# Recurrent squares summed over a sequence's four units on POOL, and over the features once per sequence on TensorE

## The chip, the cores and the metric

The kernel runs on one core of a Trainium2 chip. A core has five engines that the text names: PE (TensorE, matrix products; PEld is its weight load), DVE (VectorE), ACT (ScalarE), POOL (GpSimd) and SP (SyncE, which issues DMAs). They run their own instruction lists in order and meet only at semaphores. The metric is device time in microseconds (us), lower is better. Three runs of the kernel before took 1675.21, 1675.7 and 1678.19 us, median 1675.7. Its profiled execution has a span of 1672.1 us from the first to the last instruction.

## The reference, cut to what matters

Two sequences of 1024 tokens with 1024 features go through one layer: a layer norm, a mixer and a mixture of experts. The mixer runs attention on one half of the features and a gated linear recurrence (RG-LRU) in both directions on the other half, 512 features. The recurrence's output is normed by the root of its mean square over the 512 features, and that mean square is what the change computes in another way:

```python
h_fwd = rg_lru_scan(xc, lru_wa[0], lru_ba[0], lru_wx[0], lru_bx[0], lru_lambda[0], False)
h_bwd = rg_lru_scan(xc, lru_wa[1], lru_ba[1], lru_wx[1], lru_bx[1], lru_lambda[1], True)
lru = (h_fwd + h_bwd) * jax.nn.gelu(y_lru.astype(jnp.float32))
merged = jnp.concatenate([rms_norm(attn, attn_out_g, LN_EPS),
                          rms_norm(lru, lru_out_g, LN_EPS)], axis=-1).astype(h.dtype)
# rms_norm(x, g, eps): xf * rsqrt(mean(square(xf), axis=-1) + eps) * g
return merged @ w_out
```

## The kernel before, in words

The program runs in stages one after another: `project_xy` (input norm, projection of the recurrent half, convolution), `qkv_lru` (projection to queries, keys and values, and the recurrence), `attend`, the routing, the experts, and a last norm. The change is in `qkv_lru` (about 235 to 482 us of the profile) and in the first few instructions that `attend` does on DVE.

`qkv_lru` carries two jobs side by side. The first is the projection of 16 token tiles of 128 tokens. For a tile t, PE does `front(t)` (48 products into `pj`, lines 110 to 112), ACT copies and squares it (lines 875 to 882), DVE norms it and applies the rotary angles (lines 1018 to 1048) with POOL doing the swapped half (`swap`, line 1100), ACT and POOL split it into a high and a low part (`split`, lines 890, 891 and 1108, 1109), and PE transposes it (`back(t)`, line 829). The second job is the recurrence, in eight units: unit n is a sequence (units 0 to 3 the first, 4 to 7 the second) and one block of 128 features. The features lie on the partitions and the 1024 tokens along the free axis. PE computes the gates (line 841), ACT their tanhs and decays (lines 927 to 945), DVE does three wide products (lines 989, 996, 998), two scans (lines 1004, 1005) and the output (lines 1011, 1014), ACT squares the output into `r[n % 2][:, 1]` (`squares_of_output`, line 868), and PE sums those squares over the 128 features: `sums` (line 799) uses a 128-token piece of the squares as weights and a column of ones as the moving operand, so that the sums come out with one token per partition, 8 columns for 8 pieces. ACT copies these columns into `lru_sums` (line 864), and `attend` adds the four units of a sequence on DVE (line 1552) ahead of an inverse square root.

The order of all this is written out by hand. `GROUPS` lists nine groups g = 0 to 8: tile 0, then tiles (1, 2), (3, 4) up to (13, 14), then tile 15. In group g, PE does the fronts of its tiles, and at the end of the last front the `sums` of unit g - 2; then it does the backs of the tiles of group g - 1 and the gates of unit g. DVE in group g does the second rotation of the tiles before, the wide products and scans of unit g - 1, the norms of the group's tiles, the output of unit g - 1, and the first rotation. ACT squares the output of unit g - 1 as the last thing of group g. POOL in group g does `split` for each tile of the group before and then `swap` for each of its own. After the last group DVE scans unit 7, ACT squares its output, PE sums it (`last_sums`) and ACT copies the sums; then the stage ends, and all engines meet before `attend` starts.

Of the kernel before, what the change touches and what calls it, by code (L numbers as in the profile page):

```python
# [30 lines left out]
ALU = mybir.AluOpType  # L31
ACT = mybir.ActivationFunctionType
AX = mybir.AxisListType.X
# [81 lines left out]
def build(nc, x, ln_in_g, ln_in_b, w_in, conv_w, conv_b, lru_wa, lru_ba, lru_wx, lru_bx, lru_lambda,  # L115
# [13 lines left out]
    with ExitStack() as whole:  # L129
# [4 lines left out]
        with ExitStack() as kept:  # L134
# [3 lines left out]
            v_all = sb("v_all", [P, NT, KVW])  # L138
            lru_sums = sb("lru_sums", [P, SEQS * FT, TPS])

# [487 lines left out]
def qkv_lru(nc, raw, w_hi, w_lo, spare, q_g, k_g, rope, identr, ht_hi_dram, ht_lo_dram, k_hi, k_lo, v_all, q_dram,  # L628
# [11 lines left out]
    with ExitStack() as ctx:  # L640
# [5 lines left out]
        NU = len(UNITS)  # L646

        TILES = [NT - 1, NT - 2] + list(range(NT - 2))
        turned_last = lambda t: [v[:, 1, :].rearrange("p (j k n) -> p j k n", j=2, k=KD)[:, t % 2] for v in (k_hi, k_lo)]
# [37 lines left out]
        i = spare[:, 0:2 * SEQ].rearrange("p (d t) -> p d t", d=2)  # L687
        th = sb("lru_th", [P, 2, SEQ])

        pj = [ps(f"pj{u}", [P, 1024]) for u in range(2)]  # L690
# [39 lines left out]
        squared = sem("lru_squared")  # L730
        last_sums = sem("last_sums_done")
        block = ctx.enter_context(nc.Block())
        by_head = lambda v: v.rearrange("p (h d) -> p h d", h=NH)
# [59 lines left out]
        def _(pe):  # L793

            def sums(n, out):
                pe.wait_ge(ones_made, 1)
                pe.wait_ge(squared, n + 1)
                for c in range(TPS):
                    last = pe.matmul(out[:, SUMS + c:SUMS + c + 1], r[n % 2][:, 1, c * P:(c + 1) * P], ones[:, 0:1],
                                     start=True, stop=True)  # L800
                return last

            def front(t, unit=None):
                u = t % 2
                c = (c_hi[u], c_lo[u]) if t >= 2 else turned_last(TILES[t])
                if t >= 2:
                    pe.wait_ge(c_in[u], 32 * (t // 2))
                    pe.wait_ge(v_done, t - 1)
                for a, b in ((0, QW), (QW, QKVW)):
                    for k in range(KD):  # L810
                        last = three_pass(pe, pj[u][:, a:b], (c[0][:, k, :], c[1][:, k, :]),
                                          (w_hi[:, k, a:b], w_lo[:, k, a:b]), k == 0, k == KD - 1)
                if unit is not None:
                    last = sums(unit, pj[u])
                last.then_inc(pj_done, 1)
# [41 lines left out]
            back(NT - 1, (0, 1, 2))  # L857
            sums(NU - 1, pj[0]).then_inc(last_sums, 1)

        @block.scalar  # L860
        def _(act):

            def keep_sums(n, u):
                return act.activation(lru_sums[:, n, :], pj[u][:, SUMS:SUMS + TPS], ACT.Copy)

            def squares_of_output(n):
                act.wait_ge(out_done, n + 1)
                act.activation(r[n % 2][:, 1], ys[:], ACT.Square).then_inc(squared, 1)

            def square(t, unit=None):  # L870
                u = t % 2
                act.wait_ge(pj_done, t + 1)
                if t >= 2:
                    act.wait_ge(ss_done, t - 1)
                act.activation(sq[u], pj[u][:, 0:QKW], ACT.Square).then_inc(sq_done, 1)
                if t >= 2:
                    act.wait_ge(a_done, t - 1)
                    act.wait_ge(b_done, t - 1)
                act.activation(xr[u], pj[u][:, 0:QKW], ACT.Copy).then_inc(copied, 1)
                if unit is not None:  # L880
                    keep_sums(unit, u)
                act.activation(v_all[:, TILES[t], :], pj[u][:, QKW:QKVW], ACT.Copy).then_inc(v_done, 1)

# [33 lines left out]
            def gate_tanhs(n, pair):  # L917
# [5 lines left out]
                if not of_input and n >= 2:  # L923
                    act.wait_ge(out_done, n - 1)
                for b in (2 * pair, 2 * pair + 1):
                    act.wait_ge(gates_done, GH * n + b + 1)
# [52 lines left out]
            act.wait_ge(last_sums, 1)  # L979
            keep_sums(NU - 1, 0)  # L980
            act.wait_ge(q_stored, 16 * NT)
# [90 lines left out]
        def _(pool):  # L1072
# [31 lines left out]
            def split(t):  # L1104
# [5 lines left out]
                                   k_st[u][:, 0].bitcast(F32), ALU.subtract).then_inc(lo_done, 1)  # L1110

            for g, group in enumerate(GROUPS):
                for t in GROUPS[g - 1] if g else []:
                    split(t)
                for t in group:
                    swap(t)
# [9 lines left out]
def attend(nc, w_out, attn_g, lru_g, ln_g, ln_b, router_wg, router_bg, router_we, router_be, ident,  # L1126
# [14 lines left out]
    with ExitStack() as ctx:  # L1141
# [394 lines left out]
        def _(dve):  # L1536
# [3 lines left out]
            dve.wait_ge(ones_made, 3)  # L1540
            LRU_LINKS = 2 + RSQRT_LINKS_WIDE
            EARLY = LRU_LINKS + 1 + RSQRT_LINKS_WIDE
# [7 lines left out]
            def lru_norms():  # L1550
                link = Chain(dve, dve_link)
                link(dve.tensor_reduce(lru_tmp[:].rearrange("p (s c) -> p s c", s=SEQS),
                                       lru_sums[:].rearrange("p (s f) c -> p s c f", s=SEQS), AX, ALU.add))
                link(dve.tensor_scalar(lru_var[:], lru_tmp[:], ALPHA ** 2 / LW, LN_EPS * ALPHA ** 2, ALU.mult, ALU.add))
                rsqrt(dve, link, lru_var[:], rl[:], lru_tmp[:], wide=True)
# [1096 lines left out]
```

## Time and profile before

| what | value |
|---|---|
| median of three runs | 1675.7 us |
| span of the profiled execution | 1672.1 us |
| median less that span | 3.6 us |
| instructions in the profile | 29383 |
| busy over the span | PE 1504.5, PEld 1273.7, DVE 1096.2, ACT 912.6, POOL 491.1 us |
| granted PE clock, mean | 0.949 |

The span runs from the first instruction to the last; the 3.6 us are what the runs' median has beyond it. The busy times are averages over stages with different limits: over the whole span PE is busy for 90% and DVE for 66%, and inside `qkv_lru` the two are near each other. So the shares of the whole say little about one stage, and the rows further down are read by stage.

### The profile page before, as it was taken

Reading aid. Unit: us, or ns where it says so; the run is one execution under the profiler, and the core shown is the slowest. Engines: PE = TensorE matmul, PEld = TensorE weight load, DVE = VectorE, ACT = ScalarE, POOL = GpSimd, SP = SyncE. Lnnn points to the kernel's source line nnn. Section 1 sums busy time; section 2 is a strip of 40 time slices with the busy share of each in tenths; the row PEclk is TensorE's granted clock in tenths of the full one; section 3 lists DMA queues with packets and bytes.
Section 4 is the critical chain, followed back from the end, with each engine's and each line's share of the span. In section 5 each row is a group of like instructions: output and inputs, shape, how many; then the busy total and the mean of one; then the engine's idle time right before and its main releaser. Section 6 shows DMA issues by size and latency. Waiting matters only on the chain. (4 is left out here: it accounts for less than half of the span.)

```text
span 1672.1 us, 29383 instructions
## 1 busy us (share of the span) xinstructions
PE 1504.5 (90%) x8921; PEld 1273.7 (76%) x8923; DVE 1096.2 (66%) x2047; ACT 912.6 (55%) x1524; POOL 491.1 (29%) x343
## 2 busy tenths in 40 slices
PE   5999989999858999999999999996799999999940
PEld 5999967677747888888888888883587788777830
DVE  7787538999978776767767777767454433444237
ACT  3444437878847555555555565543365544555325
POOL 1212125565620111111111111121454353454318
PEclk9999999999959999999999999995799999999975
DMA  8855543444242111111111111116489777786566
GB/s 277 302 210 200 195 145 117 169 160 168 101 159 83 58 57 57 56 56 61 65 69 64 56 56 57 45 39 227 166 250 277 214 205 202 220 255 185 112 197 268
DMA packets 118771, 245.02 MB, mean 147 GB/s; under 512 B 18082, under 2 KB 71330, under 8 KB 118692
## 3 DMA queue, kind: packets, MB, share of 16 engines
q1 hardware_dynamic: 88752, 156.44, 26.6%
q0 software_dynamic: 12528, 45.62, 11.3%
q10 hardware_dynamic: 17412, 41.96, 6.5%
q8 instruction: 44, 0.72, 0.2%
q14 instruction: 35, 0.29, 0.0%
HBM read 149.61 MB, written 94.37 MB: 146 GB/s over the span
## 5 line engine op out<-in xcount | busy, mean ns | idle before, releaser
L1570 DVE TENSOR_TENSOR d_probs_t_lo<-d_pt_ps,d_probs_t_hi 128x512 fp32r<-128x512 f32 x256 | 164.3, 684 | 103.4 <-ACT d_probs_t_hi L1491 102.6
L1491 ACT ACTIVATE d_probs_t_hi<-d_pt_ps 128x512 fp32r<-128x512 f32 x256 | 139.3, 596 | 152.5 <-PE d_pt_ps L1347 146.1
L1713 POOL TENSOR_TENSOR d_h_tile<-d_s_tile,d_ln_g_b 128x512 f32<-128x512 f32 x30 | 38.6, 1285 | 576.7 <-ACT d_s_tile L1509 545.9
L1548 DVE TENSOR_REDUCE d_neg_max<-d_s_ps 128x1 f32<-128x1024 f32 x128 | 155.6, 1216 | 2.6 <-PE d_s_ps L1336 2.6
L110 PE MATMUL acc<-k_hi,wl_hi 128*128 128x256 f32 x512 | 146.4, 286 | 4.4 <-DVE k_lo L526 4.4
L110 PE MATMUL e_a_ps<-up_hi,e_xt_hi 128*128 x336 | 138.1, 411 | 8.3 <-DVE e_xt_lo L2358 4.2
L111 PE MATMUL acc<-k_lo,wl_hi 128*128 128x256 f32 x512 | 145.5, 284 | 0.0
L112 PE MATMUL acc<-k_hi,wl_lo 128*128 128x256 f32 x512 | 145.4, 284 | 0.0
L1474 ACT ACTIVATE d_probs<-d_s_ps,d_neg_max 128x1024 f32<-128x1024 f32 x128 | 143.3, 1119 | 3.5 <-DVE d_neg_max L1548 3.5
L1365 PE MATMUL d_ot_ps<-d_probs_t_hi,d_v_split 128*128 128x256 f32 x512 | 130.1, 292 | 8.0 <-DVE d_probs_t_lo L1570 5.8
L1347 PE MATMUL d_pt_ps<-ident,d_probs 128*128 128x128 f32 x1024 | 134.0, 274 | 3.3 <-ACT d_probs L1474 3.2
L111 PE MATMUL e_a_ps<-up_lo,e_xt_hi 128*128 x336 | 134.2, 399 | 0.0
L112 PE MATMUL e_a_ps<-up_hi,e_xt_lo 128*128 x336 | 134.1, 399 | 0.0
L1347 PEld LDWEIGHTS d_pt_ps<-ident,d_probs 128*128 128x128 f32 x1024 | 117.7, 141 | 13.2 <-ACT d_probs L1474 5.3
L1365 PE MATMUL d_ot_ps<-d_probs_t_lo,d_v_split 128*128 128x256 f32 x512 | 125.1, 282 | 0.0
L1335 PE MATMUL d_s_ps<-k_hi,d_q_tile 128*128 128x512 f32 (+1 forms) x256 | 113.2, 442 | 4.5 <-DMA d_q_tile<-q_dram 4.5
L2185 POOL DMA_INDIRECT e_xg<-h_dram,e_ix x45 | 45.1, 1003 | 225.9 <-ACT e_yt L2312 123.9
L1365 PEld LDWEIGHTS d_ot_ps<-d_probs_t_hi,d_v_split 128*128 128x128 f32 x512 | 97.3, 190 | 16.7 <-issue 16.7
L1336 PE MATMUL d_s_ps<-k_lo,d_q_tile 128*128 128x512 f32 (+1 forms) x256 | 102.4, 400 | 0.0
L110 PEld LDWEIGHTS acc<-k_hi,wl_hi 128*128 128x128 f32 x512 | 98.2, 192 | 5.0 <-DVE k_lo L526 5.0
L110 PE MATMUL d_m_ps<-d_wo_hi,d_m_hi 128*128 128x512 f32 x240 | 99.4, 414 | 0.0
L111 PEld LDWEIGHTS acc<-k_lo,wl_hi 128*128 128x128 f32 x512 | 98.3, 192 | 0.0
(394 smaller groups left out, 4040.0 us busy)
## 6 DMA issues: line engine op xcount, KB each, us to landing
up_raw<-in_exp_w SPq DMA_DIRECT2D x32, 1024.0 KB, 8.6
down_raw<-in_exp_w SPq DMA_DIRECT2D x16, 1024.0 KB, 14.0
h_dram<-v_all ACTq DMA_DIRECT2D x16, 512.0 KB, 3.4
ht_hi_dram<-k_hi ACTq DMA_DIRECT2D x8, 1024.0 KB, 4.3
ht_lo_dram<-k_lo ACTq DMA_DIRECT2D x8, 1024.0 KB, 6.8
q_dram<-wq_raw ACTq DMA_DIRECT2D x16, 512.0 KB, 3.2
d_q_tile<-q_dram SPq DMA_DIRECT2D x16, 512.0 KB, 3.7
d_h_tile<-h_dram SPq DMA_DIRECT2D x16, 512.0 KB, 3.2
```

The lines of the kernel that those rows point to most:

```text
L110: pe.matmul(out, lhs[0], rhs[0], start=first, stop=False)
L111: pe.matmul(out, lhs[0], rhs[1], start=False, stop=False)
L112: return pe.matmul(out, lhs[1], rhs[0], start=False, stop=last)
L1335: pe.matmul(out, q_t[u][:, h, :], k_hi[:, h // GQ, keys], start=True, stop=False)
L1336: last = pe.matmul(out, q_t[u][:, h, :], k_lo[:, h // GQ, keys], start=False, stop=True)
L1347: last = pe.transpose(pt_ps[c][:, j, :], pr[h % 2][:, k * P:(k + 1) * P], ident[:])
L1365: last = pe.matmul(ot_ps[:, 0:2 * P], vs[:, s * TPS + k, h // GQ].rearrange("p c d -> p (c d)"), part[:, k].rearrange("p e t -> p (e t)"), ...
L1474: act.activation(pr[h % 2][:], s_ps[h % 2][:], ACT.Exp, bias=nm[:, u, h:h + 1], accum_out=rsum[:, u, h:h + 1]).then_inc(p_done, 1)
L1491: act.activation(pt_hi[:, c * HALF:(c + 1) * HALF, h % 2], pt_ps[c][:], ACT.Copy).then_inc(pth_done[c], 1)
L1548: dve.tensor_reduce(nm[:, u, h:h + 1], s_ps[h % 2][:], AX, ALU.max, negate=True).then_inc(nm_done, 1)
L1570: dve.tensor_tensor(pt_lo[:, part, h % 2], pt_ps[c][:], pt_hi[:, part, h % 2].bitcast(F32), ALU.subtract)\
L2185: pool.indirect_dma_start(xg[u][:], None, h1_dram, bass.IndirectOffsetOnAxis(ix[u][:, 0:1], 0))\
```

## The change

The squares of a sequence's four units are added up elementwise before PE sums them over the features.

- ACT writes the squares of the first unit of each sequence (units 0 and 4) straight into a new buffer `sq_sum` of 128 x 1024, and those of the others into `r` as before.
- POOL adds the squares of units 1, 2, 3, 5 and 6 into `sq_sum` (`add_squares`), between the two splits of groups 3, 4, 5, 7 and 8.
- PE sums `sq_sum` once for the first sequence, at the end of the last front of group 5. For the second sequence, at the stage's end, each of the 8 columns takes two products, one on `sq_sum` (units 4 to 6) and one on the squares of unit 7, accumulated.
- ACT copies the sums twice in place of eight times; its writes to a buffer that POOL still has to read wait for the add. `attend` no longer adds four units (line 1552), and `lru_sums` is smaller.

```diff
+        TO_ADD = [n for n in range(NU - 1) if n % FT]
+        ADDS = [len([n for n in TO_ADD if n < FT * (seq + 1)]) for seq in range(SEQS)]
+        sq_sum = sb("lru_square_sum", [P, SEQ])
@@ tensor
-            def sums(n, out):
+            def sums(seq, out):
+                own = seq == SEQS - 1
                 pe.wait_ge(ones_made, 1)
-                pe.wait_ge(squared, n + 1)
+                pe.wait_ge(added, ADDS[seq])
                 for c in range(TPS):
-                    last = pe.matmul(out[:, SUMS + c:SUMS + c + 1], r[n % 2][:, 1, c * P:(c + 1) * P], ones[:, 0:1],
-                                     start=True, stop=True)
+                    last = pe.matmul(out[:, SUMS + c:SUMS + c + 1], sq_sum[:, c * P:(c + 1) * P], ones[:, 0:1], start=True, stop=not own)
+                    if own:
+                        if c == 0:
+                            pe.wait_ge(squared, NU)
+                        last = pe.matmul(out[:, SUMS + c:SUMS + c + 1], r[(NU - 1) % 2][:, 1, c * P:(c + 1) * P], ones[:, 0:1],
+                                         start=False, stop=True)
...
-                if unit is not None:
-                    last = sums(unit, pj[u])
+                if unit == FT - 1:
+                    last = sums(0, pj[u])
...
-            sums(NU - 1, pj[0]).then_inc(last_sums, 1)
+            sums(1, pj[0]).then_inc(last_sums, 1)
@@ scalar
             def squares_of_output(n):
                 act.wait_ge(out_done, n + 1)
-                act.activation(r[n % 2][:, 1], ys[:], ACT.Square).then_inc(squared, 1)
+                if n == FT:
+                    act.wait_ge(summed, 1)
+                act.activation(r[n % 2][:, 1] if n % FT else sq_sum[:], ys[:], ACT.Square).then_inc(squared, 1)
...
                 if not of_input and n >= 2:
                     act.wait_ge(out_done, n - 1)
+                    if n - 2 in TO_ADD:
+                        act.wait_ge(added, TO_ADD.index(n - 2) + 1)
@@ gpsimd
+            def add_squares(n):
+                pool.wait_ge(squared, n + 1)
+                if n % FT > 1:
+                    pool.wait_ge(added, TO_ADD.index(n))
+                pool.tensor_tensor(sq_sum[:], sq_sum[:], r[n % 2][:, 1], ALU.add).then_inc(added, 1)
+
             for g, group in enumerate(GROUPS):
                 for t in GROUPS[g - 1] if g else []:
                     split(t)
+                    if g - 2 in TO_ADD and t == GROUPS[g - 1][0]:
+                        add_squares(g - 2)
@@ attend, vector
-                link(dve.tensor_reduce(lru_tmp[:].rearrange("p (s c) -> p s c", s=SEQS),
-                                       lru_sums[:].rearrange("p (s f) c -> p s c f", s=SEQS), AX, ALU.add))
-                link(dve.tensor_scalar(lru_var[:], lru_tmp[:], ALPHA ** 2 / LW, LN_EPS * ALPHA ** 2, ALU.mult, ALU.add))
+                link(dve.tensor_scalar(lru_var[:], lru_sums[:].rearrange("p s c -> p (s c)"), ALPHA ** 2 / LW, LN_EPS * ALPHA ** 2, ALU.mult, ALU.add))
```

On POOL, in group 3, the order before is split of tile 3, split of tile 4 (`q_st` and `k_st` are the low parts of queries and keys), then the swaps:

```order
L1108 TENSOR_TENSOR q_st<-wq_raw,q_st 128x8x64
L1109 TENSOR_TENSOR k_st<-wq_raw,k_st 128x256
L1108 TENSOR_TENSOR q_st<-wq_raw,q_st 128x8x64
L1109 TENSOR_TENSOR k_st<-wq_raw,k_st 128x256
L1100 TENSOR_TENSOR wq_raw<-wq_raw,rope_gain 128x16x16 x2
```

After the change one instruction stands between the two splits:

```order
L1124 TENSOR_TENSOR k_st<-wq_raw,k_st 128x256
L1131 TENSOR_TENSOR lru_square_sum<-lru_square_sum,lru_r 128x1024
L1123 TENSOR_TENSOR q_st<-wq_raw,q_st 128x8x64
L1124 TENSOR_TENSOR k_st<-wq_raw,k_st 128x256
L1115 TENSOR_TENSOR wq_raw<-wq_raw,rope_gain 128x16x16 x2
```

The second split of the group is now queued behind a 128 x 1024 addition.

On PE the end of the stage before is the back of tile 15 (`tr`) and then the eight sums of unit 7, each of which the chip runs as two instructions:

```order
L829 MATMUL tr1<-identr,q_st1 128x128 x4
L829 MATMUL tr0<-identr,q_st1 128x128 x4
L829 MATMUL tr1<-identr,k_st1 128x128 x4
L799 MATMUL pj0<-ones_b,lru_r1 128x1 x8
```

After the change each column takes a pair (the first pairs and the last are shown here by three):

```order
L806 MATMUL pj0<-ones_b,lru_square_sum 128x1
L810 MATMUL pj0<-ones_b,lru_r1 128x1
L806 MATMUL pj0<-ones_b,lru_square_sum 128x1
L810 MATMUL pj0<-ones_b,lru_r1 128x1
L806 MATMUL pj0<-ones_b,lru_square_sum 128x1
L810 MATMUL pj0<-ones_b,lru_r1 128x1
```

Sixteen products stand there where eight stood, and the six other groups of eight that PE had at the ends of fronts (groups 2, 3, 4, 6, 7 and 8) are gone; the one of group 5 stays, on `sq_sum`.

## Rows read from the trace of the kernel before

**Rows 1.** Busy time by window: PE, PEld, DVE, ACT, POOL, clock, DMA share, GB/s.

```profile
300.00:325.00 25.00, 24.52 (x143) 19.99 (x142) 24.47 (x19) 20.11 (x30) 16.18 (x12) 1.00 0.46 170
```

**Rows 2.** DVE's waits from 255 to 477 us: total, times, longest.

```profile
DVE lru_th L996 <- ACT lru_th L945: 8.0, 2, 6.9
DVE wq_raw L1048 <- POOL wq_raw L1100: 3.3, 8, 1.3
```

**Rows 3.** Timeline of DVE: start, duration, line, operation, [idle before <- releaser].

```profile
294.65 1.51 DVE L1018 TENSOR_REDUCE ss<-wq_raw 128x10 f32<-128x640 f32 x2
...
314.81 2.29 DVE L998 TENSOR_TENSOR spare<-spare,lru_th 128x2048 f32<-128x2048 f32 x1
317.14 3.25 DVE L1004 TENSOR_TENSOR_SCAN lru_r<-lru_r,spare 128x1024 f32<-128x1024 f32 x1
320.31 2.74 DVE L1005 TENSOR_TENSOR_SCAN lru_r<-lru_r,spare 128x1024 f32<-128x1024 f32 x1
322.97 1.51 DVE L1018 TENSOR_REDUCE ss<-wq_raw 128x10 f32<-128x640 f32 x2
...
425.76 2.29 DVE L996 SCALAR_TENSOR_TENSOR lru_th<-lru_r,lru_th 128x2048 f32<-128x2048 f32 x1 [1.07 <-ACT lru_th L945]
...
467.90 2.29 DVE L1004 TENSOR_TENSOR_SCAN lru_r<-lru_r,spare 128x1024 f32<-128x1024 f32 x1
```

**Rows 4.** Timeline of PE: the sums, what follows them, and group 3's later parts.

```profile
288.54 1.84 PE L799 MATMUL pj<-ones_b,lru_r 128*128 128x1 f32 x16
290.24 0.85 PE L829 MATMUL tr<-identr,q_st 128*128 128x128 f32 x8
...
317.28 1.84 PE L799 MATMUL pj<-ones_b,lru_r 128*128 128x1 f32 x16
...
323.79 1.20 PE L829 MATMUL tr<-identr,q_st 128*128 128x128 f32 x8
```

**Rows 5.** Timelines of POOL and ACT in the same group.

```profile
315.15 3.09 POOL L1108 TENSOR_TENSOR q_st<-wq_raw,q_st 128x512 fp32r<-128x512 f32 x1 [4.72 <-ACT k_st L891]
318.19 2.71 POOL L1109 TENSOR_TENSOR k_st<-wq_raw,k_st 128x256 fp32r<-128x256 f32 x1
...
310.34 1.04 ACT L868 ACTIVATE lru_r<-lru_y 128x1024 f32<-128x1024 f32 x1
```

**Rows 6.** The stage before: POOL's 128x1024 adds and DVE beside them.

```profile
100.07 5.64 POOL L326 TENSOR_TENSOR v_all<-v_all,ln_in_b_b 128x1024 f32<-128x1024 f32 x2 [17.43 <-DVE v_all L522]
...
101.05 2.36 DVE L553 TENSOR_SCALAR neg_lam<-lam_t 128x8 f32<-128x8 f32 x1
103.44 2.31 DVE L554 TENSOR_TENSOR abs_lam<-lam_t,neg_lam 128x8 f32<-128x8 f32 x1
```

**Rows 7.** Lines by form: a small DVE operation alone, the last stage's POOL adds.

```profile
L94 DVE TENSOR_SCALAR ms<-ms 128x20 f32<-128x20 f32 x6 | 1.1, 176 | 0.2
...
L2610 POOL TENSOR_TENSOR up_raw<-up_raw,c_b_b 128x1024 f32<-128x1024 f32 x7 | 16.3, 2360 | 0.2
```

**Rows 8.** Timeline of the stage's end, all engines.

```profile
475.02 1.23 DVE L1014 TENSOR_TENSOR lru_y<-lru_y,lru_r 128x1024 f32<-128x1024 f32 x1
...
476.85 1.06 ACT L868 ACTIVATE lru_r<-lru_y 128x1024 f32<-128x1024 f32 x1
...
478.05 3.54 PE L799 MATMUL pj<-ones_b,lru_r 128*128 128x1 f32 x16 [1.85 <-ACT lru_r L868]
```

**Rows 9.** Timeline of the first microseconds of `attend`.

```profile
483.09 0.27 DVE L1552 TENSOR_REDUCE d_lru_tmp<-lru_sums 128x16 f32<-128x64 f32 x1
...
488.29 1.23 DVE L1548 TENSOR_REDUCE d_neg_max<-d_s_ps 128x1 f32<-128x1024 f32 x1 [2.22 <-PE d_s_ps L1336]
```

**Rows 10.** Windows around the stage's end (columns as in rows 1).

```profile
456.00:457.00 1.00, 0.19 (x2) 0.11 (x1) 1.00 (x1) 0.77 (x2) 1.00 (x2) 1.00 0.84 283
...
458.00:459.00 1.00, 0.00 (x0) 0.00 (x0) 1.00 (x2) 0.58 (x2) 1.00 (x1) 0.50 0.00 0
...
490.00:495.00 5.00, 4.11 (x14) 3.20 (x15) 5.00 (x5) 3.54 (x7) 0.00 (x0) 0.50 0.87 181
```

More of the change, by code:

```diff
@@ L138, in build @@
             v_all = sb("v_all", [P, NT, KVW])
-            lru_sums = sb("lru_sums", [P, SEQS * FT, TPS])
+            lru_sums = sb("lru_sums", [P, SEQS, TPS])
             with ExitStack() as front:
@@ L731, in qkv_lru @@
         last_sums = sem("last_sums_done")
+        added = sem("lru_squares_added")
+        summed = sem("lru_squares_summed")
         block = ctx.enter_context(nc.Block())
@@ L863, in keep_sums @@
             def keep_sums(n, u):
-                return act.activation(lru_sums[:, n, :], pj[u][:, SUMS:SUMS + TPS], ACT.Copy)
+                return act.activation(lru_sums[:, n, :], pj[u][:, SUMS:SUMS + TPS], ACT.Copy).then_inc(summed, 1)
             def squares_of_output(n):
                 act.wait_ge(out_done, n + 1)
-                act.activation(r[n % 2][:, 1], ys[:], ACT.Square).then_inc(squared, 1)
+                if n == FT:
+                    act.wait_ge(summed, 1)
+                act.activation(r[n % 2][:, 1] if n % FT else sq_sum[:], ys[:], ACT.Square).then_inc(squared, 1)
             def square(t, unit=None):
@@ L879, in square @@
                 act.activation(xr[u], pj[u][:, 0:QKW], ACT.Copy).then_inc(copied, 1)
-                if unit is not None:
-                    keep_sums(unit, u)
+                if unit == FT - 1:
+                    keep_sums(0, u)
                 act.activation(v_all[:, TILES[t], :], pj[u][:, QKW:QKVW], ACT.Copy).then_inc(v_done, 1)
@@ L979, in _ @@
             act.wait_ge(last_sums, 1)
-            keep_sums(NU - 1, 0)
+            keep_sums(1, 0)
             act.wait_ge(q_stored, 16 * NT)
@@ L1540, in _ @@
             dve.wait_ge(ones_made, 3)
-            LRU_LINKS = 2 + RSQRT_LINKS_WIDE
+            LRU_LINKS = 1 + RSQRT_LINKS_WIDE
             EARLY = LRU_LINKS + 1 + RSQRT_LINKS_WIDE
```

## The prediction

> **What bounds the kernel now.** I read busy time by window first, since the page's shares are means over stages. In the middle of the stage that the change edits, PE is busy for 24.52 of 25 us and DVE for 24.47 [rows 1]. Both look full, and PE's clock is at its full level of 2.4 GHz. Only one of them can set the pace, so I read next who waits for whom. From 255 us, where DVE takes up the products of unit 0, to 477 us DVE waits for ACT 8.0 us in two waits, of which 6.9 come at the very start, and for POOL 3.3 us in eight small ones [rows 2]. So behind the start it idles 1.1 us for ACT [rows 3] and 3.3 for POOL in over 200 us, and never for PE. The timelines give the two rates. PE's sums start 28.74 us apart (288.54 and 317.28) [rows 4]; DVE's squares start 28.32 us apart (294.65 and 322.97) [rows 3]. DVE began 6.1 us behind PE and gains a little on it in each group; once, at 425.76, it catches up and waits 1.07 us for the chain that starts at PE. PE's own lead can be read too: PE takes up tile 4's transposes at 323.79 [rows 4], while POOL has delivered them at 318.19 + 2.71 = 320.90 [rows 5], 2.9 us earlier, and POOL's delivery is paced by DVE. So the stage has two clocks that nearly agree. Take 2 to 3 us from PE and it stands at a DVE-paced handover; add to DVE and the stage's end moves by as much. At the end only DVE counts: its last output ends at 476.25, ACT squares, PE sums, ACT copies, and the stage is over [rows 8].
>
> **PE's part inside the groups.** Eight sums are 16 instructions, 1.70 us from the first to the next operation (288.54 to 290.24) [rows 4]. Six of these go, 10.2 us of PE. But PE is not what ends last there. DVE has nothing shorter in its list, and the only idle time of DVE that a faster PE and ACT take away is the 1.07 us of [rows 3]. I take -1.1 us for the removal of 10.2. The rest becomes PE's waiting: for POOL's second split of the group, and for the tanhs that wait for DVE's scans. ACT loses six copies of 8 columns each; DVE waits for ACT only in that same 1.07 us, so they are in it already.
>
> **POOL's part.** Five additions of 128 x 1024 f32. POOL itself has room for them: it stands idle 4.72 us ahead of the second split [rows 5], and an addition takes 2.36 us alone [rows 7]. ACT's squares of unit 1 are ready at 311.38 [rows 5], behind POOL's first split, so the order holds nobody up for long. What costs is DVE. Look at 314.81 to 323.05 [rows 3] beside [rows 5]. POOL's operation on 128 x 512 starts at 315.15, makes no headway until DVE's product ends at 317.10 and takes 3.09 us; the scan behind that product then takes 3.25 us, against 2.29 for a scan that meets nothing (at 467.90) [rows 3], 0.96 more. The next scan takes 2.74, 0.45 more, beside the tail of POOL's 128 x 256 operation. They don't share: one holds and the other stands still. For the size in question the trace has a direct case in the stage before. Beside two POOL adds of 128 x 1024 that take 5.64 us together, two DVE operations on 8 columns take 2.36 and 2.31 us [rows 6]; one on 20 columns alone takes 0.18 [rows 7]. Each add took 2.18 and 2.13 us from DVE. Where the five new adds would start, DVE is in its wide products, each with two operands in SBUF, and has no idle time that could take them. The last add, of unit 6 in group 8, meets DVE's small norm operations, which is the case of [rows 6] itself. I take 2.14 us each, 10.7 in all. From below the price is 0 if none of them meets DVE, and 1.92 each (twice the 0.96 of a half-size operation) by the next nearest row; from above 2.36 each, the whole add, 11.8. A gain is excluded: an add shortens nothing on DVE.
>
> The Trainium skill ("SBUF — State Buffer", section "Who interferes with whom") has a rule that speaks against this change: DVE and GpSimd share one pair of SBUF ports under an exclusive lock, and a DVE instruction with two SBUF inputs blocks, or is blocked by, a GpSimd instruction that reads SBUF, for the whole of it. The trace agrees in kind (the 0.96 us and the 2.13 us above). By the rule taken to the letter each add would cost its whole 2.36 us, 1.1 us more in the sum than by the row.
>
> **New waits.** PE's sums of the first sequence in group 5 wait for the add of unit 3, with the transposes and gates behind them. ACT's first gate tanh of groups 3, 4, 5 and 7 waits for the add; behind it stand ACT's decays, for which DVE waits later. PE's own work is now 28.7 - 1.7 = 27.0 us a group, and DVE's 28.3 + 2.1 = 30.4, so PE has 3.4 us a group to lose, and the add starts as soon as the DVE product then running ends. Both waits fit into that. I take 0. If the cover is gone, they cost what the next case below says.
>
> **The stage's end.** The last sums start when ACT has squared unit 7 [rows 8]. Before, 16 instructions followed, 3.54 us, 0.221 each, at half clock. Now two of 32 may run ahead of the wait, 30 follow: 14 more, 14 x 0.221 = 3.1 us, with nothing beside them. The bound below: the clock comes back inside the sequence, at 1.70 / 16 = 0.106 each that is 1.5 us; and since PE has then worked for longer before `attend`, whose first products still run at half clock at 490 to 495 [rows 10], it may give back 1.5 us there, so 0. I take 3.1, the row of this very place.
>
> **The first instructions of `attend`.** DVE's addition of 0.27 us goes [rows 9], but DVE waits 2.22 us for PE at 488.29, so it is hidden: 0. Were that cover gone, it would gain 0.3.
>
> **The sum.** -1.1 + 10.7 + 3.1 = +12.7 us on the profiled span of 1672.1, so 1684.8; the median lies 3.6 us above that span, and 1675.7 + 12.7 = **1688.4 us**, 0.76% slower. By the bounds: 5 x 1.92 - 1.1 + 0 = +8.5 (1684.2) to 11.8 + 3.1 = +14.9 (1690.6), the latter without the gain of 1.1.
>
> **Rivals.**
> 1. *The adds meet nobody.* They slide into moments in which DVE uses one SBUF operand, as its reductions do (1.51 us for two) [rows 3]. Then -1.1 + 3.1 = +2.0, 1677.7. For it: ACT and POOL have more slack than DVE, so the adds may settle elsewhere. Against: a reduction is shorter than an add, and POOL takes its operand as soon as it can [rows 5].
> 2. *PE is the pace after all, and the result is faster.* PE's period of 28.74 is the longer of the two [rows 3, 4]. If DVE's surplus could be made up inside its group, say because its blocked time today is due to how POOL falls against it, all of 10.2 would come back: -10.2 + 3.1 = -7.1, 1668.6. It decides from the point where an add takes less than 0.4 us from DVE, the difference of the two periods. Against it stands [rows 6].
> 3. *PE's waits lower its clock.* In [rows 10] the clock goes from full to half within 2 us of PE running dry (456 to 459). PE now waits up to 3.4 us in a group. If it runs at half clock for some 10 us of the next fronts, it loses 5, of which 3.4 are slack, so 1.6 us in each of four groups: 6.4 more, 1694.8. For it: the row. Against: the waiting comes in two pieces with transposes between, and DVE needs PE's tiles only some 10 us later. The Trainium skill ("TensorE: Matmul & The Clock Gate", section "Part 1: The HAM clock gate") says that an idle PE is put back to 1.2 GHz; rows 10 agree.
>
> **How the numbers follow.** The forecast gets 0.76, rival 1 gets 0.09, rival 2 gets 0.06, rival 3 gets 0.09. A measurement of this kernel can tell 0.2%, 3.4 us, from no change. The forecast and rival 3 are slower by more than that; rival 1 is within it; rival 2 faster. That gives faster 0.06, same 0.09, slower 0.85. The range for 8 in 10 goes from 1680, where three of the five adds are hidden and the clock comes back in the last sums (-1.1 + 4.3 + 1.5 = +4.7, 1680.4), to 1692, half way to rival 3.
>
> **What the new profile would show.** Right: DVE full from 255 us to its last output, its squares about 30.4 us apart in the four groups with adds and 28.3 in group 6; in each of the five groups one DVE operation, or two, longer by 2.1 us beside POOL's new line; POOL's add between 2.4 and 4.7 us; PE waiting 2 to 4 us a group for POOL or ACT; 32 last sums in about 7 us; the stage's end some 12 to 13 us later, and nothing changed behind it. Wrong: DVE operations of unchanged length beside the adds, squares still 28.3 apart, or DVE waiting for ACT or PE in the middle groups.

## The result and the profile after

The changed kernel takes a median of 1686.99 us (1682.68 to 1688.56, four runs), the kernel before, run beside it, 1676.49 us (1675.21 to 1678.19, four runs). The ratio is 1.0056 with an interval of 1.0039 to 1.0073: slower, by about 10.5 us. The forecast was 1688.4, or 0.76% slower, which is just above the upper end of that interval. The profiled execution has a span of 1684.6 us against the forecast's 1684.8; before it was 1672.1.

The whole time is a sum over many parts, most of which the change does not touch, so I measure the stage by itself: from DVE's first pair of squares (266.31 us before, 266.37 after) to the first ACT operation of `attend` (482.81 and 495.73). Before this is 216.50 us, after 229.36, **12.86 more; the forecast's sum was 12.7**.

DVE's timeline of the changed kernel in group 3, columns as in [rows 3]. The lines are numbered anew: L1011 is the old L996, L1013 the old L998, L1019 and L1020 the two scans, L1033 the squares.

```profile
312.59 4.48 DVE L1011 SCALAR_TENSOR_TENSOR lru_th<-lru_r,lru_th 128x2048 f32<-128x2048 f32 x1
317.11 3.25 DVE L1013 TENSOR_TENSOR spare<-spare,lru_th 128x2048 f32<-128x2048 f32 x1
320.39 2.70 DVE L1019 TENSOR_TENSOR_SCAN lru_r<-lru_r,spare 128x1024 f32<-128x1024 f32 x1
323.02 2.26 DVE L1020 TENSOR_TENSOR_SCAN lru_r<-lru_r,spare 128x1024 f32<-128x1024 f32 x1
325.20 1.51 DVE L1033 TENSOR_REDUCE ss<-wq_raw 128x10 f32<-128x640 f32 x2
```

POOL's timeline beside it: the new addition, then the second split.

```profile
311.54 3.39 POOL L1131 TENSOR_TENSOR lru_square_sum<-lru_square_sum,lru_r 128x1024 f32<-128x1024 f32 x1 [1.02 <-ACT lru_r L881]
315.23 2.98 POOL L1123 TENSOR_TENSOR q_st<-wq_raw,q_st 128x512 fp32r<-128x512 f32 x1 [0.30 <-ACT k_st L904]
318.17 2.77 POOL L1124 TENSOR_TENSOR k_st<-wq_raw,k_st 128x256 fp32r<-128x256 f32 x1
```

Read against [rows 3] and [rows 5]: the addition begins while DVE is in the product ahead, and ends at 314.93. The product behind takes 4.48 us; the operation that meets no one takes 2.29. POOL then starts its second split where it did before (315.23 against 315.15), so the split's two holds fall on the next product and the first scan instead of on the two scans. They cost the same as before: 3.25 and 2.70 where it was 3.25 and 2.74. Only the addition's hold is new. This group's squares start 30.48 us after those of group 2 (294.72), against 28.32 before. From each group to the next it is 30.48, 30.49, 30.45, 28.32 and 30.48 us up to group 7, and the one at the old distance ends in group 6, which has no addition.

In group 8 POOL's addition comes during another product, which has 2.19 us still to go, and holds the next one. First POOL's row, then DVE's:

```profile
462.91 4.39 POOL L1131 TENSOR_TENSOR lru_square_sum<-lru_square_sum,lru_r 128x1024 f32<-128x1024 f32 x1
```

```profile
465.13 4.31 DVE L1013 TENSOR_TENSOR spare<-spare,lru_th 128x2048 f32<-128x2048 f32 x1
```

Less that lead it takes 4.39 - 2.19 = 2.20 us; in group 3 the product ahead had 1.13 us to go, and 3.39 - 1.13 = 2.26. DVE's product is held 2.02 us here and 2.19 there.

DVE's waits from 255 to 490 us, as in [rows 2]. The wait of 1.07 us for ACT is gone, the one at the start and POOL's eight remain:

```profile
DVE lru_th L1011 <- ACT lru_th L960: 6.9, 1, 6.9
DVE wq_raw L1063 <- POOL wq_raw L1115: 3.3, 8, 1.2
```

PE's waits over the same stretch. PE has 10 us less to do and 12.9 us more time, and waits:

```profile
PE tr L840 <- POOL k_st L1124: 23.9, 4, 10.3
PE tr L840 <- ACT wq_raw L913: 5.3, 7, 1.6
PE gp L852 <- ACT spare L942: 4.3, 6, 1.6
...
PE pj L806 <- POOL lru_square_sum L1131: 0.2, 1, 0.2
```

None of these reaches DVE. Of the 23.9 us for POOL's `k_st`, 23.0 fall behind PE's last front, where the kernel before has 11.7; inside the groups it is 0.9 us, once. The last line is the new wait of the first sequence's sum for POOL's third addition: 0.2 us, once, at 376. PE's clock shows two dips, in windows of the length of [rows 1] (columns as there); one is below, the other in 375 to 400 us, also to 0.93:

```profile
325.00:350.00 25.00, 23.46 (x119) 18.30 (x120) 24.13 (x29) 19.98 (x30) 18.28 (x13) 0.93 0.38 139
```

The stage's end answers to [rows 8]. First DVE's last output and ACT's squares, then PE's first pairs, the last one, and ACT's copy with its wait:

```profile
484.96 1.23 DVE L1029 TENSOR_TENSOR lru_y<-lru_y,lru_r 128x1024 f32<-128x1024 f32 x1
...
485.94 0.55 PE L806 MATMUL pj<-ones_b,lru_square_sum 128*128 128x1 f32 x2
...
486.79 1.06 ACT L881 ACTIVATE lru_r<-lru_y 128x1024 f32<-128x1024 f32 x1
...
487.90 0.58 PE L810 MATMUL pj<-ones_b,lru_r 128*128 128x1 f32 x2 [1.41 <-ACT lru_r L881]
...
493.89 0.56 PE L810 MATMUL pj<-ones_b,lru_r 128*128 128x1 f32 x2
494.49 0.18 ACT L875 ACTIVATE lru_sums<-pj 128x8 f32<-128x8 f32 x1 [6.65 <-PE pj L810]
```

Two instructions run ahead, at 485.94, thirty follow from 487.90 to 494.45: 0.218 us each. ACT waited 3.72 us for the sums before and waits 6.65 now, 2.93 more. The clock stays at half over all of it and into `attend` (windows, columns as in [rows 10]):

```profile
490.00:495.00 5.00, 4.46 (x21) 4.37 (x21) 0.00 (x0) 0.18 (x1) 0.00 (x0) 0.50 0.00 0
```

### The profile page after: what moved, and what is told of

It is laid out like the page before. It is cut to its first block and busy times, and to the rows that moved or that the text cites. A ratio compares the mean times of both kernels' runs of the same rounds, so it can differ in the third digit from the quotient of the medians.

```text
span 1684.6 us, 29220 instructions
## 1 busy us (share of the span) xinstructions
PE 1502.6 (89%) x8842; PEld 1268.3 (75%) x8843; DVE 1107.0 (66%) x2046; ACT 913.6 (54%) x1518; POOL 508.8 (30%) x348
```

## The experiments

The first three take the change apart. Each is read by its stage length, from DVE's first squares to `attend`'s first ACT operation, because a change of a few us is small beside what the rest of the program does from one execution to the next (the last experiment shows it).

**The additions left out of the changed kernel.**

```diff
-                    if g - 2 in TO_ADD and t == GROUPS[g - 1][0]:
-                        add_squares(g - 2)
...
-                    if n - 2 in TO_ADD:
-                        act.wait_ge(added, TO_ADD.index(n - 2) + 1)
...
-                pe.wait_ge(added, ADDS[seq])
+                pe.wait_ge(squared, FT * seq + 1)
```

> The changed kernel without POOL's five additions and without the waits on them; the squares of units 1, 2, 3, 5 and 6 are left out of the sums, all else stays. Theory (each addition holds DVE for 2.1 us, and DVE sets the stage's end): DVE's squares come 28.3 us apart in every group, the changed kernel's 1687.0 falls by 10.7 to about 1676.3, 0.0% to 0.1% from the kernel before (what is left is the last sums' 3.1 less the 1.1 of DVE's wait). Rival (the additions cost nothing and the time comes from PE's waits and its lower clock): within 2 us of the changed kernel, 1685 to 1689.

Measured: 485.15 - 266.22 = 218.93 us, 10.43 less than with the additions; the whole 1681.37, ratio 1.0030 (1.0011 to 1.0048). In group 3 the two products are those of before:

```profile
312.44 2.28 DVE L1009 SCALAR_TENSOR_TENSOR lru_th<-lru_r,lru_th 128x2048 f32<-128x2048 f32 x1
314.75 2.29 DVE L1011 TENSOR_TENSOR spare<-spare,lru_th 128x2048 f32<-128x2048 f32 x1
```

So the five additions cost the stage 10.4 us, 2.09 each. The whole time did not fall to 1676.3 as I expected: the part behind the stage took 1197.3 us in this profile and 1188.9 in the changed kernel's. The last experiment shows that this part varies by itself.

**The additions put into the kernel before, with all its sums.**

```diff
+            def add_squares(n):
+                pool.wait_ge(squared, n + 1)
+                pool.wait_ge(added, TO_ADD.index(n) + 1)
+                pool.tensor_tensor(sq_sum[:], sq_sum[:], r[n % 2][:, 1], ALU.add).then_inc(added, 1)
...
+                    if g - 2 in TO_ADD and t == GROUPS[g - 1][0]:
+                        add_squares(g - 2)
```

> The kernel before, with all its sums on PE, plus POOL's five additions at the places where the change has them, into a buffer that nobody reads, and ACT's waits for them. Theory (DVE): DVE's squares 30.5 us apart in groups 3, 4, 5 and 7, and the time 10.7 above the kernel before less the 1.1 us wait that a later DVE no longer has: 9.6 more, 1686.1. Rival (PE's relief bought part of it back, so without it the additions cost more): 10.2 us more than that, 1696.

Measured: 491.90 - 265.47 = 226.43 us, 9.93 more than before; the whole 1687.16, ratio 1.0059 (1.0042 to 1.0076). The additions alone make nearly all of the loss, whether PE is relieved or not. The same product is held:

```profile
311.69 4.49 DVE L1001 SCALAR_TENSOR_TENSOR lru_th<-lru_r,lru_th 128x2048 f32<-128x2048 f32 x1
```

**PE's relief alone: six of the eight groups of sums left out of the kernel before.**

```diff
-                if unit is not None:
-                    last = sums(unit, pj[u])
+                if unit == FT - 1:
+                    last = sums(unit, pj[u])
```

> The kernel before, with the sums of six units left out on PE and ACT (those of units 3 and 7 stay), and no additions. Theory (DVE sets the pace, PE's 10.2 us are not on the path): DVE loses one wait of 1.07 us, the time falls by 1.1 to about 1675.4, not to be told from the kernel before. Rival (PE is the pace): 10.2 less, 1666.3.

Measured: 481.71 - 265.81 = 215.90 us, 0.60 less than before; the whole 1678.7, ratio 1.0012 (0.9996 to 1.0028), not the 1675.4 expected. Rival 2, by which PE is the pace, falls: 10.2 us of PE's work taken away are worth 0.6 of the stage. That is little more than the 0.5 us by which the kernel before repeats; against its three executions the gain is 0.60, 1.12 and 0.63 us. Where [rows 3] has the wait, at 425.76, DVE now goes from product to product, and the product ahead is held a little (2.83 us; the one at 422.40 in the profile of before took 2.29):

```profile
422.76 2.83 DVE L989 SCALAR_TENSOR_TENSOR spare<-spare,xc 128x2048 f32<-128x2048 f32 x1
425.51 2.28 DVE L996 SCALAR_TENSOR_TENSOR lru_th<-lru_r,lru_th 128x2048 f32<-128x2048 f32 x1
```

From this kernel to the one without additions the stage grows by 218.93 - 215.90 = 3.03 us. The two differ in the last sums (16 instructions against 32) and in where ACT writes two units' squares, so this is the price of the stage's end, 3.1 in the forecast.

**The additions doubled.**

```diff
+                pool.tensor_tensor(sq_sum[:], sq_sum[:], r[n % 2][:, 1], ALU.add).then_inc(halfway, 1)
+                pool.wait_ge(halfway, TO_ADD.index(n) + 1)
                 pool.tensor_tensor(sq_sum[:], sq_sum[:], r[n % 2][:, 1], ALU.add).then_inc(added, 1)
```

> The changed kernel with each of POOL's five additions done twice in a row (those squares are counted twice in the sums, and since that changes the values the routing sees, the time is read at the stage's end: from DVE's first pair of squares to the start of attention, 229.4 us in the changed kernel). Theory (an addition holds DVE for its own length less its start and end, 2.1 us): 10.7 more, 240.1, squares 32.6 us apart in groups 3, 4, 5 and 7. Rival (the second addition falls behind DVE's wide products, where POOL had nothing to do, and costs less): under 5 more.

Measured: 503.77 - 264.08 = 239.69 us, 10.33 more. Now both products of the group are held, one by each addition:

```profile
342.61 4.49 DVE L1012 SCALAR_TENSOR_TENSOR lru_th<-lru_r,lru_th 128x2048 f32<-128x2048 f32 x1
347.13 4.37 DVE L1014 TENSOR_TENSOR spare<-spare,lru_th 128x2048 f32<-128x2048 f32 x1
```

One further addition in each of the five groups costs 10.33 / 5 = 2.07 us, so the price holds for a second addition too, which falls on the next product. The whole, 1685.3 (1679.19 to 1691.92), is no measure of it: other sums send tokens to other experts, and the experts' stage was some 15 us shorter here.

**The additions replaced by two fills.** These also occupy POOL but read nothing.

```diff
-                pool.tensor_tensor(sq_sum[:], sq_sum[:], r[n % 2][:, 1], ALU.add).then_inc(added, 1)
+                pool.memset(sq_sum[:], 1.0).then_inc(halfway, 1)
+                pool.wait_ge(halfway, TO_ADD.index(n) + 1)
+                pool.memset(sq_sum[:], 1.0).then_inc(added, 1)
```

> The changed kernel with each addition replaced by two fills of the same 128 x 1024 buffer, which write SBUF and read nothing (the sums are then of constants; the time is read at the stage's end, as from DVE's first squares to the start of attention, 229.4 us in the changed kernel). A fill of 128 x 2048 took 1.80 us in the kernel before, so the two take about 1.9. Theory (DVE's second operand and POOL's reads meet at one door; Trainium skill, SBUF, Who interferes with whom: POOL operations that only write do not contend): DVE's operations keep their length, squares 28.3 us apart, 10.4 less, 219.0. Rival (any POOL operation in SBUF holds DVE for its length): 5 x 1.6 = 8 more than that, 227.

Measured: 486.83 - 265.79 = 221.04 us; the whole 1685.41, ratio 1.0046 (1.0030 to 1.0062). POOL's two fills, and DVE beside them:

```profile
339.30 0.95 POOL L1132 MEMSET lru_square_sum<- 128x1024 f32 x1 [1.01 <-ACT lru_r L882]
340.31 0.96 POOL L1134 MEMSET lru_square_sum<- 128x1024 f32 x1
```

```profile
340.36 2.28 DVE L1012 SCALAR_TENSOR_TENSOR lru_th<-lru_r,lru_th 128x2048 f32<-128x2048 f32 x1
342.68 2.29 DVE L1014 TENSOR_TENSOR spare<-spare,lru_th 128x2048 f32<-128x2048 f32 x1
```

DVE's products keep their length. Beside them the cost of the addition is thus what it reads, not that POOL is busy or that others wait for it. The Trainium skill ("SBUF — State Buffer", section "Who interferes with whom") exempts a GpSimd operation that only writes from contending with a DVE instruction with two SBUF inputs; 2.28 and 2.29 us agree with it.

My number was 2.0 us too low. DVE waits here 4.4 us for ACT behind the start, in two waits, but nothing of them is left in group 8: its squares start 192.49 us after the first ones, against 192.60 in the kernel without additions. The 2.2 us are lost behind that point. In group 8 the fills meet DVE's small norm operations, POOL first, then DVE:

```profile
458.88 0.95 POOL L1132 MEMSET lru_square_sum<- 128x1024 f32 x1
459.89 0.95 POOL L1134 MEMSET lru_square_sum<- 128x1024 f32 x1
```

```profile
459.12 0.74 DVE L1042 TENSOR_SCALAR ms<-ss 128x10 f32<-128x10 f32 x1
459.89 0.97 DVE L92 TENSOR_SCALAR tmp_qk<-ms 128x10 int32<-128x10 int32 x1
```

Each of the two ends as a fill ends; alone such an operation takes 0.17. The split behind the fills then holds the next two, at 1.20 and 0.65 us. The four span 3.66 us here and 1.48 in the kernel without additions. So a fill takes nothing from a product of two operands, but it does hold a `TENSOR_SCALAR`, which reads one tensor.

**One of DVE's reductions moved beside the addition.** In each group with an addition DVE takes the first tile's squares, a reduction of one SBUF operand, ahead of the product (rival 1 had the adds slide into such moments).

```diff
                     gated_x(g - 1)
+                    if g - 2 in TO_ADD:
+                        squares(group[0])
                     product(g - 1)
```

> The changed kernel with DVE's reduction of the group's first tile (0.8 us, one operand in SBUF) moved from behind the scans to between the first and the second wide product in groups 3, 4, 5, 7 and 8, where POOL's addition is waiting. Theory (the addition gets its turn when the product ends, and a reduction runs beside it): in groups 3, 4, 5 and 7 the second product is held 0.8 us less, squares of the second tile about 29.7 us apart, 3 us less at the stage's end, 226.4, and 1684 in all. Rival (an addition holds DVE whatever DVE does): no change, 229.4.

Measured: 492.79 - 266.33 = 226.46 us, 2.90 less than the changed kernel; the whole 1688.38, ratio 1.0065 (1.0048 to 1.0082). DVE, and POOL's addition beside it:

```profile
342.29 0.81 DVE L1033 TENSOR_REDUCE ss<-wq_raw 128x10 f32<-128x640 f32 x1
343.02 3.75 DVE L1011 SCALAR_TENSOR_TENSOR lru_th<-lru_r,lru_th 128x2048 f32<-128x2048 f32 x1
```

```profile
341.24 3.37 POOL L1134 TENSOR_TENSOR lru_square_sum<-lru_square_sum,lru_r 128x1024 f32<-128x1024 f32 x1 [1.03 <-ACT lru_r L881]
```

The reduction runs at full speed (0.81 us) while POOL adds, and the product behind it is held 1.46 us, no longer 2.19: the two engines do run together when DVE reduces one operand. Rival 1's mechanism exists. It is worth only as much as the reduction is long. The whole missed the expected 1684 by 4.4 us, with 1196.1 us behind the stage.

One operand alone does not make the difference. In group 8 of this kernel the reduction comes too early, and the addition meets the first norm operation, a `TENSOR_SCALAR` on 10 columns that takes 0.17 us alone:

```profile
462.23 4.38 POOL L1134 TENSOR_TENSOR lru_square_sum<-lru_square_sum,lru_r 128x1024 f32<-128x1024 f32 x1
464.34 2.31 DVE L1041 TENSOR_SCALAR ms<-ss 128x10 f32<-128x10 f32 x1
```

It is held 2.14 us, as much as a product.

**PE's sums of the second sequence kept apart, so that half of them can run ahead.**

```diff
-                    last = pe.matmul(out[:, SUMS + c:SUMS + c + 1], sq_sum[:, c * P:(c + 1) * P], ones[:, 0:1], start=True, stop=not own)
-                    if own:
-                        if c == 0:
-                            pe.wait_ge(squared, NU)
+                    last = pe.matmul(out[:, SUMS + c:SUMS + c + 1], sq_sum[:, c * P:(c + 1) * P], ones[:, 0:1], start=True, stop=True)
+                if own:
+                    pe.wait_ge(squared, NU)
+                    for c in range(TPS, 2 * TPS):
...
```

> The changed kernel with the last sums in another order: the eight products on the added squares stand ahead of the wait for unit 7, in columns of their own, and only the eight of unit 7 behind it; DVE adds the two sets in the next stage. Theory (behind the wait stand 30 instructions of 0.22 us where 16 stood): the last sums after ACT's last squares take 3.5 us in place of 6.6, and the time falls by 3.1 to about 1683.9. Rival (the longer work of PE is given back by a clock that is up again sooner in the next stage): within 1 us of the changed kernel.

Measured: 494.42 - 266.56 = 227.86 us, 1.50 less; the whole 1686.77, ratio 1.0071 (1.0049 to 1.0094). Half of what I expected, and the end of the stage says why:

```profile
486.20 3.53 PE L806 MATMUL pj<-ones_b,lru_square_sum 128*128 128x1 f32 x16
...
489.60 3.55 PE L810 MATMUL pj<-ones_b,lru_r 128*128 128x1 f32 x16
493.19 0.18 ACT L995 ACTIVATE lru_sums<-pj 128x16 f32<-128x16 f32 x1 [5.07 <-PE pj L810]
```

Tile 15's transposes stand ahead of the sums on PE and wait for POOL's last split, so the first sixteen instructions start only at 486.20. ACT's squares are ready at 488.1, and the sixteen still run until 489.6. I had the sums ahead of the wait, and overlooked what is ahead of the sums.

**The sums made cheap: squares and ones in bf16 in the kernel before.** ACT rounds the squares to bf16 as it writes them.

```diff
-                act.activation(r[n % 2][:, 1], ys[:], ACT.Square).then_inc(squared, 1)
+                act.activation(squares[n % 2], ys[:], ACT.Square).then_inc(squared, 1)
...
-                    last = pe.matmul(out[:, SUMS + c:SUMS + c + 1], r[n % 2][:, 1, c * P:(c + 1) * P], ones[:, 0:1],
+                    last = pe.matmul(out[:, SUMS + c:SUMS + c + 1], squares[n % 2][:, c * P:(c + 1) * P], ones_16[:, 0:1],
```

> The kernel before with the squares written in bf16, so that a product on them is one instruction and not two; no additions. Theory: the last sums are 8 instructions of 0.22 us, 1.8 less, and PE has 0.85 us less in each of seven groups, which gives back part of DVE's one wait for ACT, 0.6 less (what leaving out six sums gave): the stage 2.4 shorter, 214.1 from DVE's first squares against 216.5, and 1674.0 in all, 0.14% faster, near what can be told. Rival (PE's issue, not the number of passes, sets the last sums' time): under 1 us less.

Measured: 480.50 - 265.84 = 214.66 us, 1.84 less than before; the whole 1678.52, ratio 1.0008 (0.9994 to 1.0021). Eight sums are eight instructions now and take 0.35 us in all, also at half clock, where I had expected 0.22 each:

```profile
477.50 0.35 PE L801 MATMUL pj<-ones,lru_r 128*128 128x1 bf16 x8 [1.85 <-ACT lru_r L870]
477.89 0.18 ACT L866 ACTIVATE lru_sums<-pj 128x8 f32<-128x8 f32 x1 [0.53 <-PE pj L801]
...
480.50 1.91 ACT L1470 ACTIVATE d_v_split<-v_all 128x2048 fp32r<-128x2048 f32 x1 [2.43 <-PEq L201]
```

ACT's wait falls from 3.72 to 0.53 us, but the first operation of `attend` then waits 2.43 us where it waited 1.00: something else closes the stage, and only 1.84 of the 2.4 us come. A candidate is the DMA that stores DVE's last output. It is issued at 475.72 and lands 3.6 us later, at 479.3; with the 1.0 us that lie between ACT's copy and `attend` in the kernel before, that is 480.3. No run tests it. This is the cheap way to what the change aimed at on PE. That it is faster than the kernel before isn't shown.

**Both kernels once more, unchanged, twice.** By then the part behind the stage, which is the same in the changed kernel and in the one with the reductions moved, had taken 1188.9 us in the one and 1196.1 in the other.

> The kernel before once more, unchanged, for the spread of its own parts. From DVE's first squares pair to attend's first ACT operation it took 216.50 us, and from there to the end 1189.3. If the part behind the stage varies from one execution to the next, this one shows something else there, up to the 1197 us that experiments without a change behind the stage have shown; the stage itself repeats within 0.5 us. If each kernel has its own fixed part behind the stage, 1189.3 comes again within 1 us.

> The changed kernel once more, unchanged. Its stage took 229.36 us and the part behind it 1188.9. If the part behind varies by execution: somewhere between 1186 and 1198. If it is fixed by the kernel: 1188.9 within 1 us. Both expect the stage at 229.4 within 0.5 us, 12.9 above the kernel before.

> The kernel before a second time, unchanged: varying by execution, a third value between 1186 and 1198 behind the stage; fixed by the kernel, 1189.3 within 1 us. The stage 216.5 within 0.5 us.

> The changed kernel a second time, unchanged: varying by execution, a third value between 1186 and 1198 behind the stage; fixed by the kernel, 1188.9 within 1 us. The stage 229.4 within 0.5 us.

| execution | stage | behind the stage | span | run |
|---|---|---|---|---|
| before | 216.50 | 1189.3 | 1672.1 | |
| before, again | 217.02 | 1195.9 | 1678.4 | 1680.17 |
| before, again | 216.53 | 1195.4 | 1676.5 | 1678.25 |
| after | 229.36 | 1188.9 | 1684.6 | |
| after, again | 229.39 | 1191.7 | 1686.9 | 1688.66 |
| after, again | 229.52 | 1189.8 | 1684.3 | 1686.18 |

The stage repeats within 0.5 us; its means, 216.68 and 229.42, are 12.74 apart. The part behind varies by up to 6.6 us in one and the same kernel. That can hide the missing 2.2 us between the 12.7 and the 10.5 by which the medians differ. Whether the changed kernel also has a shorter part behind the stage isn't settled: over three executions each it takes 1190.1 us on the mean, the kernel before 1193.5. One place of the variation can be seen. ACT's wait for the DMA of `w_out`, early in `attend`, in the kernel before and in its first repetition:

```profile
ACT d_wo_hi L1498 <- DMA d_s_tile<-in_w_out: 0.2, 1, 0.2
```

```profile
ACT d_wo_hi L1498 <- DMA d_s_tile<-in_w_out: 2.0, 1, 2.0
```

With the later transfer PE and DVE run dry too, and PE's clock falls. The ten us from 20 us behind the stage, in the same two executions:

```profile
502.81:512.81 10.00, 8.13 (x56) 6.85 (x54) 8.80 (x10) 8.74 (x15) 0.00 (x0) 1.00 0.33 117
```

```profile
502.53:512.53 10.00, 6.89 (x40) 6.27 (x39) 5.69 (x7) 5.63 (x10) 0.00 (x0) 0.83 0.48 165
```

Of six executions the three with a wait of 1.4 us or more (both repetitions of the kernel before, the first of the changed one) have the clock at 0.83 there and 1191.7 or more behind the stage; the other three have 0.2 to 0.3 or no such wait, 1.00 and 1189.8 or less. In the former the twelfth maximum of `attend` (DVE `d_neg_max`) starts 49.8 to 50.9 us behind the stage, in the latter 47.1 to 47.3, so this place is worth some 3 of the 6.6 us. More lies in the experts' stage, with 45 gathers of tokens each time: from the first gather to the last it takes 420.4, 423.2 and 423.9 us in the three executions of the kernel before. The kernel with six sums left out shows that the transfer isn't all of it: it has no wait there and the clock at 1.00, but 426.9 us of experts and 1197.3 behind the stage. That the late transfer costs its 3 us is an argument from these; no run made it late on purpose, and what makes it late stays open.

## Why the prediction was right

**The sum.** Terms of the forecast beside what the runs gave for the stage:

| term | forecast | measured |
|---|---|---|
| PE's relief inside the groups | -1.1 | -0.60 (sums left out) |
| five additions | +10.7 | +10.43 (left out), +9.93 (alone), +10.33 (doubled) |
| 14 more instructions at the end | +3.1 | +3.03 (two kernels' difference), +2.93 (ACT's wait) |
| new waits | 0 | 0.2 us of PE, none of it on DVE |
| `attend`'s first addition | 0 | 0 |
| sum | +12.7 | +12.86, +12.74 over three executions each |

The differences -0.60, +3.03 and +10.43 lead from kernel to kernel, so they add up to 12.86 by construction. What supports each term apart from that is its other entry: 9.93 (which contains the gain of DVE's wait; 9.6 forecast), 10.33 and 2.93. That the profiled span came out within 0.2 us of the forecast is luck, as the repetitions with 1686.9 and 1684.3 us show; that the stage did isn't. The 3.6 us that the forecast adds from span to median are not a fixed step either: the execution of the changed kernel that was profiled took 1686.37 us, 1.8 more than its span.

**The additions.** The step that carried the forecast was to price a 128 x 1024 addition by its only relatives in the trace, two small DVE operations in another stage that were held 2.18 and 2.13 us [rows 6]. It holds for a wide product as well: 4.48 less 2.29 is 2.19. The place was right too, DVE's wide products. One detail varies and costs nothing: for unit 6 I expected the addition to meet DVE's small norm operations. In the profile shown it met the product ahead of them; in the first repetition it ran beside the reduction and held the first small operation to 1.47 us, and the stage was as long. By the rule of the Trainium skill ("SBUF — State Buffer", section "Who interferes with whom") taken to the letter, the whole 2.36 us each, five would be 11.8; the runs gave 10.4. The measurement decides, and the hold is 0.2 to 0.3 us shorter than the addition (2.02 to 2.19 us against 2.36).

**PE's relief.** That 10.2 us of PE's work are worth about one was right, the reason only in part. I took DVE's idle 1.07 us as time to be had. But in the two repetitions of the kernel before DVE idles 4.0 and 2.5 us for ACT behind the start, not 1.1, and the stage is 0.5 and 0.0 us longer. At the one place that I followed, what happens is an exchange. The first repetition, at the unit where the first profile has no wait:

```profile
364.66 2.28 DVE L989 SCALAR_TENSOR_TENSOR spare<-spare,xc 128x2048 f32<-128x2048 f32 x1
368.08 2.87 DVE L996 SCALAR_TENSOR_TENSOR lru_th<-lru_r,lru_th 128x2048 f32<-128x2048 f32 x1 [1.14 <-ACT lru_th L945]
```

and the first profile there:

```profile
365.50 3.38 DVE L989 SCALAR_TENSOR_TENSOR spare<-spare,xc 128x2048 f32<-128x2048 f32 x1
368.80 2.82 DVE L996 SCALAR_TENSOR_TENSOR lru_th<-lru_r,lru_th 128x2048 f32<-128x2048 f32 x1
```

In the one DVE waits 1.14 us for ACT, in the other L989 is 1.10 us longer. POOL's split beside them, in the same order:

```profile
364.89 3.21 POOL L1108 TENSOR_TENSOR q_st<-wq_raw,q_st 128x512 fp32r<-128x512 f32 x1 [1.08 <-ACT k_st L891]
```

```profile
365.26 1.47 POOL L1108 TENSOR_TENSOR q_st<-wq_raw,q_st 128x512 fp32r<-128x512 f32 x1 [0.61 <-ACT k_st L891]
```

In the first execution shown DVE began its product before POOL began the split; POOL stood until 366.94 and did its work while DVE waited for ACT. In the other POOL came first and DVE stood. POOL's operation needs its share once, and it takes it from an idle or from a busy DVE. So a wait of DVE read from one profile isn't time that can be won. The gain was 0.6 us against that profile, and up to 1.1 against its repetitions.

**The stage's end.** The term was 14 x 0.221; the 30 instructions took 0.218 each at half clock, and two ran ahead. The bound by which the clock comes back within the sums did not come about (0.50 up to 495), nor was anything given back in `attend`: the clock is up again in the 13th us behind the stage in both kernels, and the twelfth maximum starts 47.08 us behind it before and 47.34 after.

**New waits.** They fit into PE's slack, as forecast. The place differs: I expected PE to wait for POOL's second split, 2 to 4 us a group. The split came no later than before, and PE waits for ACT's copies of the transposes and for tanhs, at most 1.6 us at a time.

**The rivals.** Rival 1 (additions meet nobody) falls with the 4.48 us, and rival 2 (PE is the pace) with the -0.60 of the sums left out. Rival 3's mechanism did occur: twice PE's clock fell inside the groups, to 0.93 over 25 us. Both repetitions of the changed kernel have such dips between 300 and 450 us, the three executions of the kernel before none. It had no price. DVE waits for neither ACT nor PE in those groups, and the squares stay 30.45 to 30.49 apart, as in group 7 without a dip.

## What to carry to other kernels

Moving elementwise work to an idle POOL isn't free when DVE is the pace: an addition on POOL that reads SBUF takes nearly its whole own duration out of DVE's two-operand operations, and out of a small `TENSOR_SCALAR` too. A fill on POOL takes nothing from the products, but holds a `TENSOR_SCALAR`. Ask which engine sets the pace before relieving one. Then put the moved work beside its reductions, the only operations seen here to go on beside an addition, as far as they are long enough. And read a change of less than one per cent by marks around its own stage: 0.5 us of spread there against 7 in the rest.

## What was unexpected on the hardware

- A wait and a hold can take each other's place, 1.14 us of one for 1.10 of the other at the place shown. DVE's idle time behind the start of the stage is 1.1, 4.0 and 2.5 us in three executions of the same kernel, its length 216.50, 217.02 and 216.53.
- What meets POOL's addition on DVE matters by kind, not by the number of tensors read: a `TENSOR_REDUCE` of one operand keeps its 0.81 us, a `TENSOR_SCALAR` of one operand on 10 columns takes 2.31 us in place of 0.17. Even a fill, which holds no product, holds it (0.74 and 0.97 us).
- An addition of 128 x 1024 on POOL takes 2.36 us alone [rows 7], 3.39 us where the running DVE product has 1.13 us to go and 4.39 where it has 2.19. DVE loses 2.0 to 2.2 us in either case.
- A column of ones against 128 x 128 weights costs two instructions of 0.22 us in f32 at half clock, and one of 0.04 in bf16 (0.35 us for eight).
